# Attention by head pair between halves of the query tiles, with keys made once, in a two-block kernel

## The reference

```
proj = u @ w_in                      # gate 1024, recurrent 1024, q 1024, k 128, v 128
y_a = gelu(gate) * rg_lru(conv(xr))  # recurrence along the tokens
# 16 query heads of 64, 2 key/value heads (8 query heads to each)
s = q @ k.T / 8 - slope[head] * distance
# allowed: the 16 meta tokens, and the last 128 tokens (causal)
mx = max(s, sink[head]);  p = exp(s - mx)
p = p / (sum(p) + exp(sink[head] - mx))
y_b = p @ v
mix = concat(y_a, y_b) @ w_out
```

## Time and profile before

| | |
|---|---|
| median of 3 runs | 2832.0 us (2828.04 to 2836.6) |
| profiled execution, its own time | 2838.95 us |
| its span | 2837.2 us |
| mean granted clock of TensorE | 0.952 |
| TensorE busy | 2619.5 us (92%) |
| VectorE busy | 1356.5 us (48%) |
| ScalarE busy | 656.5 us (23%) |
| GpSimd busy | 699.4 us (25%) |
| HBM read | 351.10 MB |

### The profile page before, as it was taken

The page is one execution under the profiler, slowest core; times in us unless marked ns, Lnnn a source line. Parts: engine busy times, 40 slices in busy tenths (PEclk is TensorE's granted clock), DMA queues, the critical chain, the costliest instruction groups (busy, mean ns, idle before and its releaser), DMA issues.

```text
span 2837.2 us, 36655 instructions
## 1 busy us (share of the span) xinstructions
PE 2619.5 (92%) x13975; PEld 1951.5 (69%) x13975; DVE 1356.5 (48%) x2604; ACT 656.5 (23%) x1448; POOL 699.4 (25%) x658
## 2 busy tenths in 40 slices
PE   6999887789995899989899999999998999999998
PEld 3544684533332788568788888788886677888887
DVE  5574643411113441471646863414567843557832
ACT  2212221110111362551211110222226701211100
POOL 1421320011220000022043432034434630244420
PEclk9998998699998999799999999999999989999999
DMA  6233003489873112002122222122220011222222
GB/s 263 105 134 132 18 1 134 161 329 410 360 307 139 45 60 75 31 2 89 52 96 76 90 104 119 62 90 87 89 75 16 2 60 60 75 89 90 75 119 89
DMA packets 49484, 312.56 MB, mean 110 GB/s; under 512 B 12193, under 2 KB 14497, under 8 KB 18209
## 3 DMA queue, kind: packets, MB, share of 16 engines
q1 hardware_dynamic: 39520, 290.30, 26.6%
q0 software_dynamic: 9216, 17.85, 1.7%
q10 hardware_dynamic: 576, 2.10, 0.2%
HBM read 351.10 MB, written 16.78 MB: 130 GB/s over the span
## 4 chain that ended last, share of the span: by engine, by line
PE 62%; DVE 3%; ACT 1%; issue 1%; DVEq 1%; POOL 0%; ACTq 0%; POOLq 0%
PE ps L1044 33%; PE ps L533 8%; PE ps L1104 5%; PE ps L1084 4%; PE ps L1173 2%; PE ps L1081 1%; PE ps L1020 1%; PE ps L1038 1%; DVE work L1867 1%; PE ps L1006 1%; PE ps L1310 1%; PE ps L1282 1%; PE ps L1305 1%; PE ps L1318 1%; DVE work L1864 1%; DVE u L1867 1%
## 5 line engine op out<-in xcount | busy, mean ns | idle before, releaser
L533 PE MATMUL ps<-u,ring 128*128 128x264 f32 (+2 forms) x1280 | 363.0, 443 | 7.9 <-DVE u L1867 5.2
L533 PEld LDWEIGHTS ps<-u,ring 128*128 128x128 f32 x1280 | 243.7, 192 | 117.6 <-issue 82.6
L1044 PE MATMUL ps<-work,ring 128*128 128x264 f32 (+2 forms) x1172 | 274.6, 388 | 7.9 <-DVE work L1864 5.5
L1867 DVE SCALAR_TENSOR_TENSOR work<-tmp,par,work 128x528 f32<-128x528 f32 (+1 forms) x332 | 265.6, 800 | 24.7
L1864 DVE TENSOR_TENSOR work<-work 128x128 f32<-128x128 f32 (+8 forms) x461 | 238.4, 553 | 75.7 <-ACT work L1757 22.5
L1044 PEld LDWEIGHTS ps<-work,ring 128*128 128x128 f32 x1172 | 225.1, 193 | 46.2 <-DVE work L1864 6.0
L1044 PE MATMUL ps<-work 128*128 128x264 f32 (+2 forms) x1012 | 238.0, 383 | 0.0
L1044 PE MATMUL ps<-u,ring 128*128 128x264 f32 (+1 forms) x992 | 229.3, 384 | 0.0
L1044 PEld LDWEIGHTS ps<-work 128*128 128x128 f32 x1012 | 192.3, 190 | 29.8
L1044 PEld LDWEIGHTS ps<-u,ring 128*128 128x128 f32 x992 | 188.2, 190 | 30.7 <-issue 0.4
L2834 POOL TENSOR_TENSOR work<-ring 128x512 f32<-128x512 f32 (+1 forms) x46 | 68.3, 1484 | 483.5 <-PE ps L1044 356.8
(11 more groups left out here) (430 smaller groups left out, 4239.6 us busy)
## 6 DMA issues: line engine op xcount, KB each, us to landing
ring<-in_stream SPq DMA_DIRECT2D x169, 1024.0 KB, 4.9
work<-in_experts SPq DMA_DIRECT2D x25, 2048.0 KB, 13.7
work<-in_experts SPq DMA_DIRECT2D x25, 1024.0 KB, 13.9
ring<-in_experts SPq DMA_DIRECT2D x7, 2048.0 KB, 14.1
ring<-in_experts SPq DMA_DIRECT2D x7, 1024.0 KB
work<-rows_out SPq DMA_DIRECT2D x4, 1024.0 KB, 7.9
h<-in_x_fm SPq DMA_DIRECT2D x1, 2048.0 KB, 10.4
rows_in<-work ACTq DMA_DIRECT2D x4, 512.0 KB, 2.6
```

The costliest lines, as they stand in the source:

```text
L533: m = pe.matmul(ps[:, 2 * (q % 2) + half, at0:at0 + cnt], ring[:, (n + b // 16) % WSLOTS, b % 16 * P:(b % 16 + 1) * P], x[:, lo:lo + cnt], ...
L1044: m = pe.matmul(ps[:, bank, 0:n], w[kk], x[kk], start=fresh and kk == 0, stop=ends and kk == len(w) - 1, skip_group_check=not fresh)
L1867: return dve.scalar_tensor_tensor(out=out, in0=x, scalar=s, in1=y, op0=op0, op1=op1)
```

## The change

Queries wait, keys and values come first. The ring loads the units of keys and values before those of the queries (`IN0_LOADED`). The keys are made once: for each half of the tokens and each of 8 blocks, two matmuls with 64 weight columns each, key head 0 into rows 0 to 63 and key head 1 into rows 64 to 127. ACT copies head 0 to `k_fm` rows 0 to 63 and head 1 to rows 64 to 127, and two DMAs on ACT's queue copy each to the other rows. Then come the last gate products, the values, query tile 0, the transposes of the values, and the first half of query tile 1; the other thirteen halves stand in the attention's loop, at the numbers of `Q_HALVES`, in bank 3. The items go head pair by head pair, query tiles in the order 1, 2, 0, 3, 4. Scores rotate through three banks (four from item 36 on), and VectorE releases each head's bank by itself. VectorE's differences are cut at six and two tiles instead of four and four. The counts of `half_done` and `half_read` in later stages are shifted by 7, ACT's and POOL's lists follow the new order, and SP's loads of `in0` are written out instead of looped.

```diff
@@ -94,8 +94,12 @@
+def _lru_kv_q(u):
+    return 2 * (u + 1) if u < 9 else 2 * u + 1
...
-          ("in0", 14, 27, lambda u: min(2 * (u + 1), 27)), ("out0", 8, 8, _pairs),
+          ("in0", 14, 27, _lru_kv_q), ("out0", 8, 8, _pairs),
@@ -115,6 +119,11 @@
+IN0_LOADED = [U0["in0"] + u for u in [*range(8), 12, 13, *range(8, 12)]]
+ATT = [(c, hp) for hp in range(Q_TILES) for c in (1, 2, 0, 3, 4)]
+Q_HALVES = dict(zip((-1, 0, 1, 4, 6, 9, 11, 14, 16, 19, 21, 24, 26, 29), [(t, s) for t in range(1, Q_TILES) for s in range(2)]))
+SCORE_BANK = [(2 * n + e) % 3 if n < 36 else 2 * (n % 2) + e for n in range(len(ATT)) for e in range(2)]
+SCORE_FREE = [max([0] + [i + 1 for i in range(n) if SCORE_BANK[i] == SCORE_BANK[n]]) for n in range(len(SCORE_BANK))]
@@ -403,7 +412,8 @@
-                sp.dma_start(ring[:, slot, :], a["stream"][n]).then_inc(sem(f"unit_loaded{slot}"), 16)
+                m = IN0_LOADED[n - U0["in0"]] if U0["in0"] <= n < U0["out0"] else n
+                sp.dma_start(ring[:, slot, :], a["stream"][m]).then_inc(sem(f"unit_loaded{slot}"), 16)
@@ -957,29 +967,33 @@
-            for t in range(2 * LRU, 2 * LRU + Q_TILES + 3):
-                in0(t)
-                if t == 2 * LRU:
-                    lru_gates(LRU - 1)
...
             def scores(n):
...
-                if n >= 2:
-                    pe.wait_ge(sem("scores_read"), n - 1)
+                if n == 0:
+                    pe.wait_ge(sem("lru_loaded"), 64)
+                pe.wait_ge(sem("tile_read"), q0 + 2 * LRU + 3 + hp + 1 + 2)
                 for e in range(2):
+                    if SCORE_FREE[2 * n + e]:
+                        pe.wait_ge(sem("scores_read"), SCORE_FREE[2 * n + e])
                     rows = slice(64 * e, 64 * e + 64)
-                    out = ps[0:cnt, 2 * (n % 2) + e, :]
+                    out = ps[0:cnt, SCORE_BANK[2 * n + e], :]
@@ -1023,10 +1037,43 @@
+            unit_wait(n0 + 8)
+            pe.wait_ge(sem("tile_read"), q0 + 2 * LRU + 1)
+            for s in range(2):
+                for k in range(DT):
+                    for e in range(2):
+                        b = (n0 + 8) % WSLOTS, P * (DT * e + k)
+                        m = pe.matmul(ps[HEAD * e:HEAD * (e + 1), 2 * ((q0 + 2 * LRU) % 2) + s, 0:HALF],
+                                      ring[:, b[0], b[1]:b[1] + HEAD], u[:, k, s * HALF:(s + 1) * HALF],
+                                      start=(k == 0), stop=(k == DT - 1), tile_position=(0, HEAD * e))
+            m.then_inc(sem("tile_done"), 2)
+            lru_gates(LRU - 1)
...
+            def query_half(t, s):
+                if s == 0:
+                    if t % 2 == 0:
+                        unit_wait(n0 + 10 + t // 2)
+                    pe.wait_ge(sem("tile_read"), q0 + 2 * LRU + 3 + t + 2)
+                else:
+                    pe.wait_ge(sem("half_read"), t)
+                for k in range(DT):
+                    b = P * (DT * (t % 2) + k)
+                    m = pe.matmul(ps[:, 3, 0:HALF], ring[:, (n0 + 10 + t // 2) % WSLOTS, b:b + P],
+                                  u[:, k, s * HALF:(s + 1) * HALF], start=(k == 0), stop=(k == DT - 1))
+                m.then_inc(sem("tile_done" if s else "half_done"), 1)
...
+            v_turned()
+            query_half(*Q_HALVES[-1])
             scores(0)
             for n in range(len(ATT) + 2):
                 if n + 1 < len(ATT):
                     scores(n + 1)
+                if n in Q_HALVES:
+                    query_half(*Q_HALVES[n])
                 if 1 <= n <= len(ATT):
                     turn(n - 1)
@@ -1607,19 +1654,30 @@
+            act.wait_ge(sem("tile_done"), q + 2)
+            act.activation(halves(k_fm[0:HEAD, 0, :]), pair2(q)[0:HEAD], ACT.Copy)
+            act.activation(halves(k_fm[HEAD:P, 1, :]), pair2(q)[HEAD:P], ACT.Copy).then_inc(sem("tile_read"), 2)
+            act.wait_ge(sem("tile_read"), q + 4)
+            act.dma_start(k_fm[HEAD:P, 0, :], k_fm[0:HEAD, 0, :]).then_inc(sem("lru_loaded"), 16)
+            act.dma_start(k_fm[0:HEAD, 1, :], k_fm[HEAD:P, 1, :]).then_inc(sem("lru_loaded"), 16)
+            lru_functions(LRU - 1)
...
@@ -1630,6 +1688,8 @@
+                if n and n - 1 in Q_HALVES:
+                    query_copy(*Q_HALVES[n - 1])
@@ -2472,8 +2531,8 @@
-                    m.then_inc(sem("scores_read"), 1)
+                        stt(prob[0:cnt, b, e, 1:1 + nk], dist, slope(2 * hp + e), ps[0:cnt, SCORE_BANK[2 * n + e], 0:nk], mul, sub
+                            ).then_inc(sem("scores_read"), 1)
@@ -2602,10 +2661,10 @@
-            for k in (0, OK // 2):
+            for k, w in ((0, OK - 2), (OK - 2, 2)):
                 dve.wait_ge(sem("lru_out"), LRU)
-                dve.wait_ge(sem("attended_read"), len(ATT) - OK // 2 + k)
+                dve.wait_ge(sem("attended_read"), len(ATT) // OK * (k + w))
```

More of the change, by code:

```diff
@@ L417, in stream_rest @@
                 trips = max(units, 0) // WSLOTS
-                if trips > 1 and stage != "in1":
+                if trips > 1 and stage not in ("in1", "in0"):
                     per = ENDED[n0][1] - ENDED[n0 - WSLOTS][1]
@@ L959, in _, with in0_heads, v_turned @@
                     lru_gates(i - 1)
-            for t in range(2 * LRU, 2 * LRU + Q_TILES + 3):
-                in0(t)
-                if t == 2 * LRU:
-                    lru_gates(LRU - 1)
-            pe.wait_ge(sem("tile_read"), q0 + 27 + 2)
-            pe.wait_ge(sem("lru_sig"), LRU)
-            for c, (lo, n) in enumerate(CH2):
-                m = pe.transpose(ps[0:n, 4 + c // 4, c % 4 * P:(c % 4 + 1) * P], v_fm[:, lo:lo + n], ident)
-            m.then_inc(sem("router_done"), 1)
-            ATT = [(c, hp) for c in range(len(CH2)) for hp in range(Q_TILES)]
+            def in0_heads(t, n, block, free):
+                pe.wait_ge(sem("tile_read"), free)
+                for s in range(2):
+                    for k in range(DT):
+                        m = pe.matmul(ps[:, 2 * ((q0 + t) % 2) + s, 0:HALF], block(ring[:, n % WSLOTS, :], k),
+                                      u[:, k, s * HALF:(s + 1) * HALF], start=(k == 0), stop=(k == DT - 1))
+                m.then_inc(sem("tile_done"), 1)
+            def v_turned():
+                pe.wait_ge(sem("tile_read"), q0 + 2 * LRU + 3 + 2)
+                pe.wait_ge(sem("lru_sig"), LRU)
+                for c, (lo, n) in enumerate(CH2):
+                    m = pe.transpose(ps[0:n, 4 + c // 4, c % 4 * P:(c % 4 + 1) * P], v_fm[:, lo:lo + n], ident)
+                m.then_inc(sem("router_done"), 1)
             def scores(n):
@@ L1578, in _, with tile_copy @@
             q0 = Q0["in0"]
-            def tile_copy(q, out, func=ACT.Copy, scale=1.0):
+            def tile_copy(q, out, func=ACT.Copy, scale=1.0, bank=None):
                 act.wait_ge(sem("tile_done"), q + 1)
-                act.activation(halves(out), pair2(q), func, scale=scale).then_inc(sem("tile_read"), 1)
+                act.activation(halves(out), pair2(q if bank is None else bank), func, scale=scale).then_inc(sem("tile_read"), 1)
             def lru_functions(i):
@@ L1609, in _, with query_copy @@
                     lru_functions(i - 1)
-            for t in range(Q_TILES):
-                tile_copy(q0 + 2 * LRU + t, q_fm[:, t, :], scale=HEAD ** -0.5)
-                if t == 0:
-                    lru_functions(LRU - 1)
-            for t in range(2):
-                tile_copy(q0 + 24 + t, k_fm[:, t, :])
-            tile_copy(q0 + 26, v_fm)
+            q = q0 + 2 * LRU
+            act.wait_ge(sem("tile_done"), q + 2)
[5 more added lines that the diff above has]
+            lru_functions(LRU - 1)
+            tile_copy(q + 2, v_fm, bank=q + 1)
+            def query_copy(t, s):
+                if s:
+                    act.wait_ge(sem("tile_done"), q + 3 + t + 1)
+                else:
+                    act.wait_ge(sem("half_done"), t)
+                act.activation(q_fm[:, t, s * HALF:(s + 1) * HALF], ps[:, 3, 0:HALF], ACT.Copy, scale=HEAD ** -0.5
+                               ).then_inc(sem("tile_read" if s else "half_read"), 1)
+            tile_copy(q + 3, q_fm[:, 0, :], scale=HEAD ** -0.5, bank=q)
             act.wait_ge(sem("router_done"), 2)
@@ L1621, in _ @@
             act.activation(v_tok[:, 4, :], ps[:, 5, 0:P], ACT.Copy).then_inc(sem("v_read"), 1)
-            ATT = [(c, hp) for c in range(len(CH2)) for hp in range(Q_TILES)]
+            query_copy(*Q_HALVES[-1])
             for n in range(len(ATT) + 2):
@@ L2603, in pairs_added @@
                     squares_added(n, 2 * p + 1)
[L2605 removed]
+            for k, w in ((0, OK - 2), (OK - 2, 2)):
                 dve.wait_ge(sem("lru_out"), LRU)
[L2607 to L2608 removed]
+                dve.wait_ge(sem("attended_read"), len(ATT) // OK * (k + w))
+                m = differences(t_out0[:, :, k:k + w, :], mix0[:, k:k + w, :], mix0[:, OK + k:OK + k + w, :], 0)
             m.then_inc(sem("terms_ready"), 1)
@@ L2816, in _ @@
                     gather_expert(2 * s + 7)
```

(3 more changed lines are left out.)

13 lines of the change are left out of this document (9 added, 4 removed).

## The result

The changed kernel takes 2814.18 us in the median of 7 runs (2808.51 to 2823.11), beside 2833.68 us for the kernel before (7 runs, 2828.04 to 2836.78). The ratio is 0.9929, 95% interval 0.9917 to 0.9942, a gain of 16.4 to 23.5 us, 19.5 in the middle. The forecast was 2807.8 us (24.2 less), the range 2799 to 2825.

The account below looks back on a forecast made before the run. TensorE was taken as the bound, VectorE close behind. Attention apart from the halves falls from 99.4 to 82.3 us, 17.1 less; with 7.1 for keys 24.2 less, giving 2807.8 us against the median, range 2799 to 2825.

Parts of the forecast that it names:

- What bounds the kernel: Whole kernel: TensorE is busy for 92% of the span, so work or waits taken off it are time.
- Keys once: Key tiles before the attention: 32 side-by-side pairs cost one tile, 7.1 us, so 7.1 us are gone.
- Drain: Changes of tiling mode on TensorE: 0.06 us each, some ten new ones, 0.6 us by the rule, left out.
- Copies of the keys: Two DMAs on ACT's queue before the first scores: hidden, landing after 2.6 us, two issues costing 0.1 us.
- Cover by the halves: Attention loops: fourteen query halves of 3.56 us, 49.8 us, are moved there as cover, no work saved.
- Rival D: Heads with halves: the cover doesn't work, 11.2 instead of 9.5 us a head, 10 us more, 2818; chance 0.09.
- Heads 0 to 5: Attention's first six heads: TensorE sets the pace, 9.5 us a head beside 7.1 of halves, 57 us, full clock.
- Start: Attention's start: halves cover TensorE's 2.81 us idle but for about 0.8, the third half waiting for ACT's copy.
- Heads 6 and 7: Last two heads, without halves: VectorE sets the pace, 11.2 us a head, 22.5 us for two.
- Tail: VectorE's differences after the attention: 16.25 us stays; cutting them six and two gains nothing.
- rival A: Heads 6 and 7: the low clock returns, up to 15.6 us more for the two, 2823; chance 0.13.
- Rivals B and E: B: low clock through the whole attention, 2930 us, chance 0.04; E: change does not show, 2832 us, chance 0.04.

Follow-up runs that it names:

- keys twice: Changed kernel with the keys made as two full doubled tiles, copied by ACT alone without DMAs; 2819.24 us, ratio 0.9947 against the kernel before.
- half behind the transposes: Changed kernel with each query half moved from before the transposes to behind them; 2819.09 us, ratio 0.9952 against the kernel before.
- queries first, new order: Changed kernel with all eight query tiles made before the attention, items still head pair by head pair; 2825.53 us, ratio 0.9978 against the kernel before.
- the old order: Changed kernel with all query tiles before the attention, items query tile by query tile, differences four and four; 2828.48 us, ratio 0.9986 against the kernel before.
- later halves: Changed kernel with the halves spread wider, the last at n = 25, 28 and 31; 2819.19 us, ratio 0.9944 against the kernel before.
- earlier sums: Changed kernel with three of GpSimd's four first weight sums moved into its loop, at n = 16, 19 and 21; 2815.17 us, ratio 0.9933 against the kernel before.
- the later series: Changed kernel repeated unchanged, 5 runs, beside a kernel with half of VectorE's differences in its loop; 2813.60 us, ratio 0.9921 against the kernel before.

## Why the prediction was right, point by point

- **What bounds the kernel.** Right: work off TensorE and gaps closed in front of it came out as time, 23.8 us in the stage where 24.2 were forecast.
- **Keys once.** 7.1 forecast, 7.1 by *keys twice*; 32 pairs take 7.27 us in the chain.
- **Drain.** Priced at 0.06 and left out. Wrong in size where it could be seen alone, 0.2 us behind the key pairs. Ten of them would be 2 us. Of the 3.2 us that the heads took too long (below) 1.1 lie in the halves themselves and could hold some of it, but no run separates it there.
- **Copies of the keys.** Hidden, as forecast, but both sizes were off: landing took 4.5 us instead of 2.6, and ACT lost 1.27 us to two issues where I had put 0.1. The 0.1 had no row behind it: in the trace of the kernel before, the issues on ACT's queue took 0.33 to 0.35 us each. The queue's lines, from the view of the DMAs between 1060 and 1110 us and from ACT's timeline:

```profile
work<-work ACTq DMA_DIRECT2D x2, 132.0 KB, 4.5
```

```profile
1076.07 0.52 ACTq L1662 DMA_DIRECT2D work<-work  x1
1076.62 0.61 ACTq L1663 DMA_DIRECT2D work<-work  x1
1077.31 1.28 ACT L1636 ACT_TABLE_LOAD   x1 [1.27 <-issue]
```

  It cost nothing because the first scores came some 19 us after the issue. The earlier trace rows was a poor model for more than its size: that transfer goes from SBUF to HBM, these two from SBUF to SBUF in 64 rows each, and the ring's loads of weights arrived at the same time (434 GB/s in all from 1077 to 1078 us). Which of these makes the 4.5 us no run shows.
- **Cover by the halves.** Right in kind: the waits of TensorE in the loops are a few tenths a head, and *half behind the transposes* shows that this is the place's doing, 8.1 us of it. Rival D is out: its loops would have taken 11.2 us a head, and they took 9.92.
- **Heads 0 to 5: the term that was mis-sized.** A head with two halves takes 17.25 us (five in a row, 1110.42 to 1196.66), not 16.6. The two halves are 7.33 us, not 7.1. The loops are 9.92, not 9.5: tiles 3 and 4 took 2.56 each as forecast, tile 2 took 2.59 (2.38), tile 1 1.71 (1.5) and tile 0 0.50 (0.45). I had halved the times of tile 1 at half clock, but at full clock its scores, transposes and products take 0.45, 0.53 and 0.73 us, each more than half of 0.78, 0.95 and 1.25. Of the excess of tile 2, 0.15 us is a wait for ACT's copy (`L1702`). Five such heads are 3.2 us.
- **Start.** 42.9 us from the origin to the first of these heads, where the forecast leaves 45.1 (155.5 less five heads of 16.6, a half, and 23.8 for the end). The third half waited 0.4 us for ACT and not 0.8. Most of the rest is where the line is drawn, since only four loops lie in front of it, and no merit of the forecast. It hides most of the point above in the total.
- **Heads 6 and 7.** A head without halves takes 11.32 us (transposes at 1204.30 to transposes at 1215.62), 11.2 forecast. From the end of the last half to the first difference it is 24.7 us; 22.5 and 1.3 forecast. The meeting of GpSimd's sum and a scaling came as forecast, on a smaller item: 1.71 us in place of 0.36, ending at 1221.54 with the sum ending at 1221.37. The Trainium skill, SBUF — State Buffer (SBUF: two separate sides), has GpSimd and some of VectorE's instructions share a port pair under an exclusive lock: whichever starts first keeps it for its whole instruction, and the other blocks. The trace agrees: the scaling ends 0.17 us behind the sum.
- **Tail.** VectorE's 16.2 us as forecast. But from first difference to mark it is 19.9 us, before 21.7: 1.7 us that I hadn't counted. Before, TensorE stood idle for 5.55 us behind its first 32 products, and from the start of the next 16 to the mark it was 5.4 us; now the 32 are slow and end about when the differences do, and the 16 behind them take 3.7 us to the mark. That part of the gain is luck for the forecast: it comes with the low clock of rival A, and no run separates it from the other cut of the differences.
- **Rival A** came true in small. The clock held through head 6 and until the last items of head 7, 3 us before the first difference. It fell between the products at 1221.73 us and the transposes at 1223.88, around two waits of 1.21 and 1.11 us, and was back at about 1236. Most of it hides under VectorE's tail. What makes it fall just there was not tested; later halves and earlier sums did not keep it up. The Trainium skill, TensorE: Matmul & The Clock Gate (What's actually happening), has activity release the throttle: that fits 1236 here and 1156 in *queries first, new order*, and it doesn't by itself explain the 20 us in which the old order had TensorE busy for 10.00 of 10 us at 0.50.
- **Rivals B and E** are out: 129 us from the keys to 1196.66 ran at 1.00, and the interval of the ratio ends at 0.9942.
- **The number.** From origin to first difference it is 22.0 us less (179.6 to 157.5) where 24.2 was forecast, 2.2 short; with 1.7 from the tail the stage is right to 0.4, so part of the agreement is two errors that cancel. The median says 19.5 us, in the later series 22.3 (2835.94 less 2813.60). The stage of the changed kernel is 177.5 us in both of its profiles, so the difference between the two is probably scatter outside of the stage; the kernel before has only one profile.

## What to carry to other kernels

Independent dense work is worth most in the place where an engine waits for a round trip through another one: here the same 50 us of matmuls cost 13.2 us more in a block of their own, and 8.1 us more behind the transposes, than in front of them. Where such work is spread, look at what remains without it (the last heads, the start of the next stage): here the low clock returned there, and halves as late as n = 31 did not keep it away. And measure a stage from a mark in front of it to one behind it: the origin lies up to 11 us apart between profiles, more than most of the edits here are worth.

## What was not expected of the hardware

- Two matmuls of 64 weight columns side by side run in the time of one of 128 (64 records in 7.27 us), and the first full-size matmuls behind them lose 0.2 us.
- A 132 KB copy from SBUF to SBUF, with weights arriving beside it, landed after 4.5 us, a 512 KB one from SBUF to HBM after 2.6.
- GpSimd's sums and VectorE's differences slow each other: the sums behind the first take 4.00, 3.73 and 3.91 us in place of 2.35, and VectorE's eight differences 16.2 in place of 10.1.

```profile
1226.76 4.00 POOL L2896 TENSOR_TENSOR work<-work,ring 128x1024 f32<-128x1024 f32 x1 [5.39 <-issue]
1230.90 3.73 POOL L2900 TENSOR_TENSOR con<-ring,work 128x1024 f32<-128x1024 f32 x1
1234.59 3.91 POOL L2936 TENSOR_TENSOR work<-ring 128x1024 f32<-128x1024 f32 x1
```
